# Eight experts' products: weight blocks or token tiles as the stationary operand of TensorE

## The chip, the cores and the metric

The kernel runs on one core of a Trainium2 chip. Its time is device time in microseconds (us) of one launch; lower is better. TensorE (PE) multiplies a stationary operand, which a LDWEIGHTS instruction puts into the array first (PEld), by a moving operand that is streamed through it column by column, and writes the sums to the eight PSUM banks of 128 x 512 float32. VectorE (DVE), ScalarE (ACT) and GpSimd (POOL) do the rest, and SyncE (SP) issues most transfers. All data are float32. In the trace each float32 product stands as two LDWEIGHTS and two MATMUL records with the same shapes: two halves of one product.

## The reference

Three layers run one after the other on 256 tokens of width 1024. The change touches only the mixture of experts of the second layer: a router picks two of eight experts for each token, each expert is a gated network with 3584 hidden columns, and the results come back weighted.

```
def moe_swiglu(h, w_router, b_router, w_gate, w_up, w_down):
    logits = (t @ w_router).astype(jnp.float32) + b_router.astype(jnp.float32)
    top_v, top_e = lax.top_k(logits, TOP_K)
    gate = jax.nn.softmax(top_v, axis=-1)
...
    def one(args):
        xb, e = args
        return (jax.nn.silu(xb @ w_gate[e]) * (xb @ w_up[e])) @ w_down[e]
```

The matrices of one expert are gate and up, 1024 x 3584 each, and down, 3584 x 1024. With eight experts that is most of what the kernel reads.

## The kernel before, in words

Each expert has CAP = 96 token slots, three groups of 32 (GRP = 3). Weights pass through a ring of six slots of 2 MB (slabs). SP issues a slab's transfer as soon as TensorE has freed the slot it goes to (issue, line 164), always in the order in which TensorE uses them; TensorE waits for a slab at its first use (slab). All of TensorE's products in this stage are issued by the helper mm, so they carry line 183.

For each expert TensorE runs two waves: 16 blocks of 128 hidden columns, then 12 (for the last expert 11; the block left over is computed in a loop of steps at the end, which also takes the tokens beyond 96 slots). A wave is expand for gate (banks 0 to 2), then expand for up (banks 3 to 5). The order for an expert is gate and up of wave 0, gate and up of wave 1, contract (down) of wave 0, locate (two products that find which tokens the next expert takes), contract of wave 1.

In expand the stationary operand is a 128 x 32 tile of tokens, moe_he, and the moving operand is a strided run of up to 512 weight columns (chunk). Four such products, one for each quarter of the array's columns (cg), write four quarters of the partitions of a bank. The result has tokens and weight columns mixed so that VectorE's 32 x 32 transposes can turn it: VectorE multiplies silu(gate) by up into moe_act (line 2784) and transposes that into moe_actT (line 2788). In contract moe_actT, 128 x 32, is again stationary, and 256 columns of down weights move, four quarters beside each other, into banks 6 and 7.

ScalarE applies silu (line 2629), copies bank 6 out (line 2619) and stores the expert's rows in four transfers (line 2622). VectorE copies bank 7 out (line 2673). The next expert's tokens come by locate, three small VectorE steps that end in the index (lines 2663 to 2665), an indirect transfer issued by GpSimd (line 2861), and three transposes into moe_he (line 2655); TensorE waits for them (he_ready) before the next expert's first product. During expert 0 four batches of spread products (moe_rows) are put between the phases and copied out by ScalarE.

The order of the work is that of the code: no planner sets it. The code of the stage is the function experts:

Of the kernel before, what the change touches and what calls it, by code (L numbers as in the profile page):

```python
# [19 lines left out]
P = 128  # L20
# [2171 lines left out]

def plan_experts(m):
# [12 lines left out]


class Experts:
# [3 lines left out]
    def __init__(self, m, ctx):  # L2212
# [20 lines left out]
        self.slot = sb("slot", [P, GRP])  # L2233
        self.pos, self.g = sb("pos", [P, TT, 8]), sb("g", [P, TT, 8])
        self.count = sb("count", [1, 8])
        self.rowT = sb("rows", [8, 2, T])
# [3 lines left out]
        self.selT = sb("selT", [P, GRP, T])  # L2240
        self.he = sb("he", [P, 2, GRP, KD, 32])
        self.sg = sb("silu", [P, GRP, 512])
        self.act = sb("act", [P, GRP, 512])
        self.actT = [sb(f"actT{w}", [P, GRP, nb, 32]) for w, (b0, nb) in enumerate(WAVES)]
        self.ye = sb("ye", [P, GRP, T])
# [157 lines left out]
class Routes:  # L2403
# [3 lines left out]
    def __init__(self, m, x, ctx):  # L2407
# [5 lines left out]
        self.diag = x.selT[:, 0:TT, 0:P]  # L2413
# [6 lines left out]
def experts(m, x, prep, router, rt):  # L2420
# [4 lines left out]
    G, U, DN = m.bank[0:3], m.bank[3:6], m.bank[6:8]  # L2425
    SC, LAST_SC = [m.bank[i] for i in range(4)], [m.bank[i] for i in range(4, 8)]
    chunk = lambda ap, cg, nb: ap.rearrange("p (b c r) -> p c b r", c=4, r=32)[:, cg]
    gath, he_ready, g_ready, sg_ready, u_ready, mul_done, at_ready, d_done, ye_ready, sc_ready, added, sel_ready, selT_ready, \
# [8 lines left out]
    a = m.a  # L2437

# [4 lines left out]
    half = GRP * 2  # L2443
    with nc.Block() as block:
        @block.tensor
        def _(pe):
# [56 lines left out]
            def scatter(e):  # L2503
                pe.wait_ge(ye_ready.sem, 2 * (e + 1))
                pe.wait_ge(selT_ready.sem, 1)
                for hf in range(2):
                    for g in range(GRP):
                        for cg in range(4):
                            r = slice(32 * cg, 32 * cg + 32)
                            end = hf == 1 and g == GRP - 1 and cg == 3  # L2510
                            m.mm(pe, LAST_SC[cg][:, hf * T:(hf + 1) * T], x.ye[r, g, hf * P:(hf + 1) * P], x.selT[r, g, :],
                                 g == 0, g == GRP - 1, sc_ready if end else None, skip_group_check=True)

            def spread(n):

                for j in range(4):
                    e = (n % 2) * 4 + j
                    m.mm(pe, DN[j // 2][:, (j % 2) * T:(j % 2 + 1) * T], m.onehot[0:8, e, :], x.rowT[:, n // 2, :], True, True,
                         sp_ready if j == 3 else None)
# [14 lines left out]
            for i, src in enumerate((x.pos, x.g)):  # L2534
                for t in range(TT):
                    c = i * T + t * P
                    m.mm(pe, m.bank[6][0:8, c:c + P], src[:, t, :], m.ident[:], True, True,
# [3 lines left out]
            for e in range(N_EXPERTS):  # L2541
                pe.wait_ge(he_ready.sem, e + 1)
                expand("eg", e, 0, G, g_ready)
                if e == 0:
                    pe.wait_ge(rows_out.sem, 1)
                    pe.wait_ge(rt.rb_out.sem, 1)
                    spread(0)
                expand("eu", e, 0, U, u_ready)
                if e == 0:
                    pe.wait_ge(sp_out.sem, 1)  # L2550
                    spread(1)
                pe.wait_ge(sg_ready.sem, half * e + GRP)
                expand("eg", e, 1, G, g_ready)
                if e == 0:
                    pe.wait_ge(sp_out.sem, 2)
                    spread(2)
                pe.wait_ge(mul_done.sem, half * e + GRP)
                expand("eu", e, 1, U, u_ready, 0, 2)
                if e == 0:
                    pe.wait_ge(sp_out.sem, 3)  # L2560
                    spread(3)
                expand("eu", e, 1, U, u_ready, 2, 4)
                if e == 0:
                    pe.wait_ge(sp_out.sem, 4)
                else:
                    pe.wait_ge(ye_ready.sem, 2 * e)
                pe.wait_ge(at_ready.sem, half * e + GRP)
                contract(e, 0)
                pe.wait_ge(mul_done.sem, half * e + half)
                pe.wait_ge(sg_ready.sem, half * e + half)  # L2570
                if e + 1 < N_EXPERTS:
                    locate(e + 1)
                if e == LAST:
                    bring()
                pe.wait_ge(at_ready.sem, half * e + half)
# [18 lines left out]
        def _(act):  # L2594
            def spread_out(n):
                act.wait_ge(sp_ready.sem, n + 1)
                for j in range(2):
                    ins = act.activation(x.spread[:, n // 2, (n % 2) * 4 + 2 * j:(n % 2) * 4 + 2 * j + 2, :],
                                         DN[j][:].rearrange("p (e n) -> p e n", e=2), ACT.Copy)
                ins.then_inc(sp_out.sem, 1)  # L2600
# [12 lines left out]
            act.activation(x.rowT[:], m.bank[6][0:8, :].rearrange("p (a n) -> p a n", a=2), ACT.Copy).then_inc(rows_out.sem, 1)  # L2613
            for e in range(N_EXPERTS):
                if e:
                    act.wait_ge(d_done.sem, e)
                    if e >= 2:
                        act.wait_ge(written.sem, 64 * (e - 1))
                    act.activation(x.ye[:, 0:2, :], DN[0][:].rearrange("p (g n) -> p g n", g=2), ACT.Copy).then_inc(ye_ready.sem, 1)  # L2619
                    act.wait_ge(ye_ready.sem, 2 * e)  # L2620
                    for cg in range(4):
                        act.dma_start(x.y_rows[(e - 1) * CAP:e * CAP, cg * T:(cg + 1) * T].rearrange("(g r) n -> r g n", r=32),
                                      x.ye[32 * cg:32 * cg + 32]).then_inc(written.sem, 16)
                for w, (b0, nb) in enumerate(waves(e)):
                    act.wait_ge(g_ready.sem, 2 * e + w + 1)
                    if e or w:
                        act.wait_ge(mul_done.sem, half * e + GRP * w)
                    for g in range(GRP):
                        act.activation(x.sg[:, g, 0:32 * nb], G[g][:, 0:32 * nb], ACT.Silu).then_inc(sg_ready.sem, 1)  # L2629
                    if e == 0:  # L2630
                        spread_out(2 * w)
                        spread_out(2 * w + 1)
# [5 lines left out]
            act.wait_ge(written.sem, 64 * LAST)  # L2638
            act.activation(x.ye[:, 0:2, :], DN[0][:].rearrange("p (g n) -> p g n", g=2), ACT.Copy).then_inc(ye_ready.sem, 1)
# [5 lines left out]
        def _(v):  # L2645
# [22 lines left out]
            def combine(e):  # L2668

                v.wait_ge(d_done.sem, e + 1)  # L2670
                if e:
                    v.wait_ge(written.sem, 64 * e)
                v.tensor_copy(x.ye[:, 2, :], DN[1][:, 0:T]).then_inc(ye_ready.sem, 1)
                if e < LAST:
                    return
                v.wait_ge(sp_out.sem, 4)
                for g in range(GRP):
                    ins = v.scalar_tensor_tensor(out=x.selT[:, g, :], in0=x.spread[:, 0, e, :], scalar=x.slot[:, g:g + 1],
                                                 in1=x.spread[:, 1, e, :], op0=ALU.is_equal, op1=ALU.mult)
                ins.then_inc(selT_ready.sem, 1)  # L2680
# [34 lines left out]
            def plan_steps():  # L2715

                wide = lambda ap: ap.rearrange("p (a c) -> p a c", a=1).broadcast_to([1, N_EXTRA, N_EXPERTS])
                nf = D_FFE // P
                v.memset(x.rank[:], 1.0)
# [52 lines left out]
            for e in range(N_EXPERTS):  # L2772
# [5 lines left out]
                for w, (b0, nb) in enumerate(waves(e)):  # L2778
                    v.wait_ge(u_ready.sem, 2 * e + w + 1)
                    if e or w:  # L2780
                        v.wait_ge(at_ready.sem, half * e + GRP * w)
                    for g in range(GRP):
                        v.wait_ge(sg_ready.sem, half * e + GRP * w + g + 1)
                        v.tensor_tensor(x.act[:, g, 0:32 * nb], x.sg[:, g, 0:32 * nb], U[g][:, 0:32 * nb], ALU.mult)\  # L2784
                            .then_inc(mul_done.sem, 1)
                    for g in range(GRP):
                        v.wait_ge(mul_done.sem, half * e + GRP * w + g + 1)
# [1457 lines left out]
```

## Time and profile before

| what | value |
|---|---|
| time, median of 3 runs | 2288.18 us (2286.75 to 2290.34) |
| time of the profiled execution | 2291.82 us |
| its span, first to last instruction | 2290.1 us |
| mean granted TensorE clock | 0.985 of full speed |
| PE, PEld busy | 2216.6 us (97%), 1579.4 us (69%) |
| DVE, ACT, POOL busy | 883.7 us (39%), 393.3 us (17%), 169.4 us (7%) |
| read from HBM | 532.94 MB |

The expert stage runs from about 858 to 1756 us of the span. PE's busy time is the union of its matmuls' spans. A matmul's span is longer than the distance from its start to the next one's, since matmuls are pipelined, so what a matmul costs in a stream is the distance from start to start, and a mean span does not tell it. The busy time of a group divided by its count comes near to that distance.

### The profile page before, as it was taken

How to read it: one execution, taken by the hardware profiler on the slowest of the kernel's cores; microseconds unless marked ns; L12 is line 12 of the kernel's file. 1: busy time of each engine (PE TensorE's matmuls, PEld its weight loads, DVE VectorE, ACT ScalarE, POOL GpSimd, SP SyncE). 2: the span in 40 equal slices, each digit the busy share in tenths (PEclk: the TensorE clock that was granted, in tenths of full speed). 3: DMA queues.
4: the chain of work that ended last, by engine and by line, in shares of the span. 5: the costliest groups of instructions: out<-in, count | busy, mean ns of one | idle time of the engine just before them, and what ended most of it. 6: DMA issues, size and time to landing. Idle time of an engine off the chain costs nothing. (4 is left out here: it accounts for less than half of the span.)

```text
span 2290.1 us, 49032 instructions
## 1 busy us (share of the span) xinstructions
PE 2216.6 (97%) x22096; PEld 1579.4 (69%) x22096; DVE 883.7 (39%) x1657; ACT 393.3 (17%) x822; POOL 169.4 (7%) x250
## 2 busy tenths in 40 slices
PE   8999999999999999999999999999998999899998
PEld 7699889998689973535353534344446877689997
DVE  2676455452566431010000100111013374768764
ACT  0242311100233320000000010000001342224302
POOL 1000100000000012000000000000001162400000
PEclk9999999999999999999999999999999997899999
DMA  7423354434333377999999999999997211055440
GB/s 248 148 93 130 122 210 158 162 129 166 111 108 123 102 276 281 403 387 393 416 411 417 413 411 414 409 415 408 415 404 261 94 38 39 10 189 187 148 182 20
DMA packets 170559, 540.96 MB, mean 236 GB/s; under 512 B 17068, under 2 KB 35022, under 8 KB 153966
## 3 DMA queue, kind: packets, MB, share of 16 engines
q1 hardware_dynamic: 154144, 528.81, 60.0%
q10 hardware_dynamic: 14622, 4.16, 0.8%
q0 software_dynamic: 1584, 4.85, 0.5%
q8 instruction: 174, 2.85, 0.5%
q14 instruction: 35, 0.29, 0.0%
HBM read 532.94 MB, written 4.85 MB: 235 GB/s over the span
## 5 line engine op out<-in xcount | busy, mean ns | idle before, releaser
L183 PE MATMUL bank<-ring,moe_he 128*32 128x512 f32 (+2 forms) x6144 | 577.7, 537 | 2.8 <-DMA ring<-in_moe_w_up 2.7
L183 PEld LDWEIGHTS bank<-ring,moe_he 128*32 128x32 f32 x6144 | 198.7, 110 | 376.6 <-issue 367.7
L183 PE MATMUL bank<-hT,ring 128*128 128x128 f32 (+1 forms) x1952 | 290.7, 307 | 9.7 <-PEq L932 3.4
L183 PE MATMUL bank<-ring,moe_actT 128*32 128x256 f32 x5352 | 292.3, 379 | 1.3 <-DMA ring<-in_moe_w_down 1.3
L183 PEld LDWEIGHTS bank<-hT,ring 128*128 128x128 f32 x1952 | 263.4, 191 | 33.4 <-issue 8.8
L183 PEld LDWEIGHTS bank<-ring,moe_actT 128*32 128x32 f32 x5352 | 174.1, 110 | 116.9 <-issue 3.9
L2784 DVE TENSOR_TENSOR moe_act<-moe_silu,bank 128x512 f32<-128x512 f32 (+2 forms) x48 | 26.8, 614 | 540.4 <-PE bank L183 540.4
L183 PE MATMUL bank<-ring 128*128 128x128 f32 (+2 forms) x976 | 121.8, 284 | 1.4 <-ACT ring L826 1.4
L183 PEld LDWEIGHTS bank<-ring 128*128 128x128 f32 (+1 forms) x976 | 115.8, 190 | 4.0 <-ACT ring L826 1.8
L183 PE MATMUL bank<-kept,ring 128*128 128x256 f32 (+1 forms) x448 | 96.6, 378 | 6.1 <-PEq L1709 3.0
L183 PEld LDWEIGHTS bank<-kept,ring 128*128 128x128 f32 x448 | 83.2, 198 | 18.5 <-issue 5.4
L2629 ACT ACTIVATE moe_silu<-bank 128x512 f32<-128x512 f32 (+2 forms) x48 | 22.6, 542 | 410.7 <-PE bank L183 410.7
L183 PE MATMUL bank<-ffn_sums,ring 128*128 128x128 f32 x768 | 88.4, 275 | 0.0
L183 PE MATMUL bank<-cffn_sums,ring 128*128 128x128 f32 x768 | 88.4, 275 | 0.0
L183 PEld LDWEIGHTS bank<-ffn_sums,ring 128*128 128x128 f32 x768 | 87.0, 192 | 0.0
L183 PEld LDWEIGHTS bank<-cffn_sums,ring 128*128 128x128 f32 x768 | 87.0, 192 | 0.0
L2861 POOL DMA_INDIRECT ring<-h_rows,moe_index x21 | 20.2, 960 | 723.5 <-DVE moe_index L2665 719.2
L1630 DVE TENSOR_TENSOR ring<-ring 128x1024 f32<-128x1024 f32 (+1 forms) x52 | 59.3, 1159 | 19.6 <-PE bank L183 18.2
L2619 ACT ACTIVATE moe_ye<-bank 128x512 f32<-128x512 f32 x7 | 4.2, 598 | 346.7 <-PE bank L183 346.7
L1636 DVE TENSOR_TENSOR ring<-ring 128x1024 f32<-128x1024 f32 (+1 forms) x52 | 59.4, 1161 | 9.8 <-PE bank L183 8.8
L1633 DVE TENSOR_TENSOR ring<-ring 128x1024 f32<-128x1024 f32 (+1 forms) x52 | 59.2, 1158 | 0.5
L183 PE MATMUL bank<-merged,ring 128*128 128x256 f32 x256 | 56.1, 380 | 0.0
(841 smaller groups left out, 2553.1 us busy)
## 6 DMA issues: line engine op xcount, KB each, us to landing
ring<-in_moe_w_down SPq DMA_DIRECT2D x55, 2048.0 KB, 19.1
ring<-in_moe_w_gate SPq DMA_DIRECT2D x32, 2048.0 KB, 23.2
ring<-in_moe_w_up SPq DMA_DIRECT2D x32, 2048.0 KB, 22.8
ring<-in_w_in SPq DMA_DIRECT2D x29, 2048.0 KB, 8.0
ring<-in_moe_w_gate SPq DMA_DIRECT2D x28, 1536.0 KB, 18.1
ring<-in_moe_w_up SPq DMA_DIRECT2D x28, 1536.0 KB, 14.6
ring<-in_w_up SPq DMA_DIRECT2D x10, 2048.0 KB, 11.9
ring<-in_w_out SPq DMA_DIRECT2D x6, 2048.0 KB, 7.9
```

The costliest lines, as they stand in the source:

```text
L183: ins = pe.matmul(out, lhsT, rhs, start=start, stop=stop, **kw)
L1630: return v.tensor_tensor(self.t3, self.b[1, 1], self.b[0, 1], ALU.subtract)
L1633: return v.tensor_tensor(self.b[0, 1], self.b[0, 1], self.b[0, 0], ALU.subtract)
L1636: return v.tensor_tensor(self.t2, self.t3, self.b[0, 0], ALU.add)
L2619: act.activation(x.ye[:, 0:2, :], DN[0][:].rearrange("p (g n) -> p g n", g=2), ACT.Copy).then_inc(ye_ready.sem, 1)
L2629: act.activation(x.sg[:, g, 0:32 * nb], G[g][:, 0:32 * nb], ACT.Silu).then_inc(sg_ready.sem, 1)
L2784: v.tensor_tensor(x.act[:, g, 0:32 * nb], x.sg[:, g, 0:32 * nb], U[g][:, 0:32 * nb], ALU.mult)\
L2861: g.indirect_dma_start(x.picked[:, j, :], None, x.rows_of_h, bass.IndirectOffsetOnAxis(ap=x.index[:, e % 2, j:j + 1], axis=0)).then_inc(pi ...
```

## The change

The token slots and the weights change places in expand. A block of 128 x 128 weights is now stationary, and the 96 token slots move, so the result has hidden columns on the partitions and 96 slots along the row: the layout that down needs, with no transpose. Four blocks fill 384 columns of a bank (PIECE = 4). Wave 0 needs four banks each for gate and up, so bank 6 joins gate and bank 7 joins up, and the products into gate's fourth bank wait until the previous expert's results have been copied out (ye_ready). In contract a tile of 128 columns of moe_actT (96 slots and 32 columns that belong to the next block, or zeros at the end) is stationary, and 512 columns of down weights move, twice for a block. The results are plain rows of 1024, stored with one transfer. The spread products of expert 0 are gathered in two places and use eight half-filled steps of other banks. The last scatter uses the whole array, and its mask is one VectorE instruction where it was three.

```
+    G, U, DN = m.bank[0:3] + m.bank[6:7], m.bank[3:6] + m.bank[7:8], m.bank[6:8]
...
-                        for g in range(GRP):
-                            for cg in range(4):
-                                end = k == KD - 1 and g == GRP - 1 and cg == 3
-                                m.mm(pe, banks[g][32 * cg:32 * cg + 32, 0:32 * nb], x.he[:, e % 2, g, k, :],
-                                     chunk(s[:, kk, :], cg, nb), k == 0, k == KD - 1, ready if end else None,
-                                     skip_group_check=True)
+                        for b in range(nb):
+                            if key == "eg" and e and k == 0 and b // PIECE == 3 and b % PIECE == 0:
+                                pe.wait_ge(ye_ready.sem, 2 * e)
+                            c = b % PIECE * CAP
+                            m.mm(pe, banks[b // PIECE][:, c:c + CAP], s[:, kk, b * P:(b + 1) * P], x.he[:, e % 2, :, k, :],
+                                 k == 0 and c == 0, k == KD - 1, ready if k == KD - 1 and b == nb - 1 else None,
+                                 skip_group_check=True)
...
-                    for g in range(GRP):
-                        for cg in range(4):
-                            first, last = w == 0 and b == 0, w == 1 and b == nb - 1
-                            end = last and g == GRP - 1 and cg == 3
-                            m.mm(pe, DN[g // 2][32 * cg:32 * cg + 32, (g % 2) * T:(g % 2 + 1) * T], x.actT[w][:, g, b, :],
-                                 s[:, b % 4, cg * T:(cg + 1) * T], first and g % 2 == 0, last, d_done if end else None,
-                                 skip_group_check=True)
+                    for h in range(2):
+                        first, last = w == 0 and b == 0, w == 1 and b == nb - 1
+                        m.mm(pe, DN[h][:], x.actT[w][:, b * CAP:b * CAP + P], s[:, b % 4, h * 512:(h + 1) * 512], first, last,
+                             d_done if last and h else None, skip_group_check=True)
...
-                    for g in range(GRP):
-                        v.wait_ge(mul_done.sem, half * e + GRP * w + g + 1)
-                        v.transpose(x.actT[w][:, g, 0:nb, :].rearrange("p b n -> p (b n)"), x.act[:, g, 0:32 * nb])\
-                            .then_inc(at_ready.sem, 1)
+                    for i, b in enumerate(range(0, nb, PIECE)):
+                        n = min(PIECE, nb - b) * CAP
+                        v.wait_ge(sg_ready.sem, pieces(e, w - 1) + i + 1)
+                        v.tensor_tensor(x.actT[w][:, b * CAP:b * CAP + n], x.silu[:, b:b + n // CAP, :].rearrange("p b n -> p (b n)"),
+                                        U[i][:, 0:n], ALU.mult).then_inc(mul_done.sem, 1)
```

On PE, experts 0 and 1 read like this before (-) and now (+). The last two numbers are the columns of the stationary and of the moving operand, and x96 counts products in a row; moe_he and moe_actT are the token tiles, ring holds the weights, moe_sel is locate, and moe_rows is the spread.

```order
+L183 MATMUL bank<-moe_he,ring 128x96 x448
+L183 MATMUL bank<-moe_rows,onehot 128x256 x6
+L183 MATMUL bank<-ring,moe_actT 128x512 x32
 L183 MATMUL bank<-moe_sel,ring 128x96 x2
-L183 MATMUL bank<-ring,moe_actT 32x256 x144
-L183 MATMUL bank<-ring,moe_he 32x512 x192
-L183 MATMUL bank<-ring,moe_he 32x384 x192
-L183 MATMUL bank<-ring,moe_actT 32x256 x192
+L183 MATMUL bank<-moe_rows,onehot 128x256 x10
+L183 MATMUL bank<-ring,moe_actT 128x512 x24
+L183 MATMUL bank<-moe_he,ring 128x96 x448
+L183 MATMUL bank<-ring,moe_actT 128x512 x32
```

An expert's 384 expand products of 128 x 32 tiles are now 448 with a 128 x 128 block each, and the 336 down products, 192 of wave 0 and 144 of wave 1, are 56 with 512 moving columns, 32 and 24. The two locate products stand where they stood.

On DVE, where TensorE's phases are waited for, the rows of expert 2 before are these:

```order
L2784 TENSOR_TENSOR moe_act<-moe_silu,bank 128x512 x3
L2788 STREAM_TRANSPOSE moe_actT<-moe_act 128x512 x3
L2795 TENSOR_SCALAR moe_sel<-moe_iota,moe_pos 128x96 x2
L2784 TENSOR_TENSOR moe_act<-moe_silu,bank 128x384 x3
L2788 STREAM_TRANSPOSE moe_actT<-moe_act 128x384 x3
```

And these are the rows of the same expert now, down to the copy of its results:

```order
L2775 TENSOR_TENSOR moe_actT<-moe_silu,bank 128x384 x4
L2782 TENSOR_SCALAR moe_sel<-moe_iota,moe_pos 128x96 x2
L2775 TENSOR_TENSOR moe_actT<-moe_silu,bank 128x384 x3
L2657 TENSOR_TENSOR moe_found<-bank,moe_diag 128x96
L2658 TENSOR_REDUCE moe_where<-moe_found 128x3
L2659 TENSOR_SCALAR moe_index<-moe_where,moe_part 128x3
L2649 STREAM_TRANSPOSE moe_he<-ring 128x256 x3
L2667 COPY moe_ye<-bank 128x512
```

The transposes into moe_actT are gone, the products with silu come in seven pieces of 384 columns where they were six, and the copy of the down results is 512 columns wide where it was 256.

## Rows read from the trace of the kernel before

**Rows 1.** The page: PE in 40 slices of the span, its clock, the DMA engines.
```profile
PE   8999999999999999999999999999998999899998
PEclk9999999999999999999999999999999997899999
DMA  7423354434333377999999999999997211055440
```

**Rows 2.** Windows view, expert stage: busy us (instructions) by engine; PEclk, DMA share, GB/s.
```profile
core 0: us, PE busy (x) PEld busy (x) DVE busy (x) ACT busy (x) POOL busy (x), PEclk, DMA share, GB/s
1000.00:1700.00 700.00, 697.19 (x9162) 298.82 (x9156) 69.51 (x182) 29.09 (x55) 20.83 (x22) 1.00 1.01 408
```

**Rows 3.** Waits of PE in the stage, by what ended them: us, times, longest.
```profile
PE bank L183 <- DMA ring<-in_moe_w_up: 2.7, 2, 1.5
PE bank L183 <- DMA ring<-in_moe_w_down: 1.3, 3, 0.5
```

**Rows 4.** Timeline of PE, expert 2: start us, us, engine, operands, stationary, moving, count.
```profile
1084.54 72.34 PE L183 MATMUL bank<-ring,moe_he 128*32 128x512 f32 x768
1156.70 20.90 PE L183 MATMUL bank<-ring,moe_actT 128*32 128x256 f32 x384
1177.53 0.69 PE L183 MATMUL bank<-moe_sel,ring 128*128 128x96 f32 x4
1178.15 15.75 PE L183 MATMUL bank<-ring,moe_actT 128*32 128x256 f32 x288
1193.71 6.62 PE L183 MATMUL bank<-ring,moe_he 128*32 128x512 f32 x60
```

**Rows 5.** PE by form, whole span: stationary, moving, count, busy us, mean ns.
```profile
L183 PE MATMUL bank<-ring,moe_he 128*32 128x512 f32 x3072 | 332.0, 592 | 2.8 <-DMA ring<-in_moe_w_up 2.7
L183 PE MATMUL bank<-cffn_sums,ring 128*128 128x128 f32 x768 | 88.4, 275 | 0.0
```

**Rows 6.** Windows view, the last dense layer, where whole 128 x 128 tiles are stationary.
```profile
2070.00:2235.00 165.00, 165.00 (x1481) 165.00 (x1480) 121.49 (x201) 41.33 (x86) 0.00 (x0) 1.00 0.45 160
```

**Rows 7.** PE by form in that window (groups cover 1477 of its 1481).
```profile
L183 PE MATMUL bank<-cffn_sums,ring 128*128 128x128 f32 x680 | 78.4, 275 | 0.0
L183 PE MATMUL bank<-hT,ring 128*128 128x128 f32 x400 | 46.5, 275 | 0.0
L183 PE MATMUL bank<-cffn_act,ring 128*128 128x128 f32 x237 | 28.4, 275 | 0.0
L183 PE MATMUL bank<-cffn_act_sums,ring 128*128 128x128 f32 x160 | 18.8, 275 | 0.0
```

**Rows 8.** Timeline of PE: 8 columns moving; 512 columns moving; the last scatter.
```profile
851.02 0.59 PE L2528 MATMUL bank<-route_mask,ones 128*128 128x8 f32 x4
...
59.62 13.04 PE L183 MATMUL bank<-ring,hT 128*128 128x512 f32 x30
...
1755.84 2.87 PE L183 MATMUL bank<-moe_selT,moe_ye 32*128 32x256 f32 x48
```

**Rows 9.** Timeline of DVE at the end of expert 3.
```profile
1287.43 0.26 DVE L2663 TENSOR_TENSOR moe_found<-bank,moe_diag 128x96 f32<-128x96 f32 x1 [18.41 <-PE bank L183]
1298.46 1.10 DVE L2655 STREAM_TRANSPOSE moe_he<-ring 128x256 f32<-128x256 f32 x3 [10.22 <-DMA ring<-h_rows,moe_index]
1303.19 0.42 DVE L2673 COPY moe_ye<-bank 128x256 f32<-128x256 f32 x1 [0.17 <-PE bank L183]
```

**Rows 10.** DVE by form, 1000 to 1700 us: the products that read a bank.
```profile
L2784 DVE TENSOR_TENSOR moe_act<-moe_silu,bank 128x512 f32<-128x512 f32 x21 | 13.2, 683 | 282.2 <-PE bank L183 282.2
```

**Rows 11.** Slab transfers issued from 1100 to 1650 us: count, KB, median us to landing.
```profile
ring<-in_moe_w_down SPq DMA_DIRECT2D x35, 2048.0 KB, 19.9
ring<-in_moe_w_gate SPq DMA_DIRECT2D x20, 2048.0 KB, 24.2
ring<-in_moe_w_up SPq DMA_DIRECT2D x20, 1536.0 KB, 14.7
```

**Rows 12.** Windows view, before and after the clock fell in the last layer.
```profile
1896.30:1903.10 6.80, 6.18 (x89) 5.21 (x90) 4.61 (x12) 2.83 (x8) 6.23 (x7) 1.00 0.01 2
1903.10:1916.70 13.60, 13.60 (x106) 9.94 (x103) 6.03 (x14) 2.38 (x9) 2.90 (x4) 0.50 0.01 2
```

More of the change, by code:

```diff
@@ L2190, in waves, with pieces @@
     return WAVES if e < N_EXPERTS - 1 else (WAVES[0], (16, 11))
+PIECE = 4
+PIECES = sum(-(-nb // PIECE) for _, nb in WAVES)
+def pieces(e, w):
+    return PIECES * e + sum(-(-nb // PIECE) for _, nb in WAVES[:w + 1])
 def plan_experts(m):
@@ L2232, in __init__ @@
         self.second = spare[:, 2 * D:3 * D]
-        self.slot = sb("slot", [P, GRP])
+        self.slot = sb("slot", [P, 1])
         self.pos, self.g = sb("pos", [P, TT, 8]), sb("g", [P, TT, 8])
         self.count = sb("count", [1, 8])
-        self.rowT = sb("rows", [8, 2, T])
+        self.rowT = sb("rows", [P, 2, T])
         self.spread = sb("spread", [P, 2, N_EXPERTS + 1, T])
@@ L2437, in experts @@
     a = m.a
+    SPREAD = (0, 1, 2, 0, 1, 2, 3, 5)
     def count(eng):
@@ L2505, in scatter, with spread @@
                 pe.wait_ge(selT_ready.sem, 1)
-                for hf in range(2):
-                    for g in range(GRP):
[L2508 to L2519, printed above, removed]
+                for c in range(KD):
+                    m.mm(pe, LAST_SC[c // 2][:, c % 2 * T:(c % 2 + 1) * T], x.ye[:, c * P:(c + 1) * P], x.selT[:], True, True,
+                         sc_ready if c == KD - 1 else None)
+            def spread(units):
+                for u in units:
+                    for j in range(2):
+                        m.mm(pe, m.bank[SPREAD[u]][:, j * T:(j + 1) * T], m.onehot[:, u % 4 * 2 + j, :], x.rowT[:, u // 4, :],
+                             True, True, sp_ready if j else None)
             pe.wait_ge(rt.consts.sem, 1)
@@ L2546, in _ @@
                     pe.wait_ge(rt.rb_out.sem, 1)
-                    spread(0)
                 expand("eu", e, 0, U, u_ready)
-                if e == 0:
[L2550 to L2558, printed above, removed]
+                pe.wait_ge(sg_ready.sem, pieces(e, 0))
+                expand("eg", e, 1, G, g_ready)
+                pe.wait_ge(mul_done.sem, pieces(e, 0))
+                expand("eu", e, 1, U, u_ready)
+                pe.wait_ge(sg_ready.sem, pieces(e, 1))
+                if e == 0:
+                    spread(range(3))
+                    pe.wait_ge(pads_zero.sem, 3)
+                contract(e, 0)
+                pe.wait_ge(mul_done.sem, pieces(e, 1))
+                if e + 1 < N_EXPERTS:
+                    locate(e + 1)
                 if e == 0:
                     pe.wait_ge(sp_out.sem, 3)
[L2561 to L2572, printed above, removed]
+                    spread(range(3, len(SPREAD)))
                 if e == LAST:
                     bring()
-                pe.wait_ge(at_ready.sem, half * e + half)
                 contract(e, 1)
@@ L2594, in _, with spread_out @@
         def _(act):
[L2595 to L2600, printed above, removed]
+            def spread_out(u):
+                act.wait_ge(sp_ready.sem, u + 1)
+                e = u % 4 * 2
+                act.activation(x.spread[:, u // 4, e:e + 2, :], m.bank[SPREAD[u]][:].rearrange("p (e n) -> p e n", e=2),
+                               ACT.Copy).then_inc(sp_out.sem, 1)
             for q in range(4):
@@ L2612, in _ @@
             act.wait_ge(rows_ready.sem, 1)
-            act.activation(x.rowT[:], m.bank[6][0:8, :].rearrange("p (a n) -> p a n", a=2), ACT.Copy).then_inc(rows_out.sem, 1)
+            act.wait_ge(pads_zero.sem, 1)
+            act.activation(x.rowT[0:8], m.bank[3][0:8, :].rearrange("p (a n) -> p a n", a=2), ACT.Copy).then_inc(rows_out.sem, 1)
             for e in range(N_EXPERTS):
@@ L2617, in _ @@
                     if e >= 2:
[L2618 to L2619 removed]
+                        act.wait_ge(written.sem, 16 * (e - 1))
+                    act.activation(x.ye[:, 0:512], DN[0][:], ACT.Copy).then_inc(ye_ready.sem, 1)
                     act.wait_ge(ye_ready.sem, 2 * e)
[L2621 to L2623 removed]
+                    act.dma_start(x.y_rows[(e - 1) * CAP:e * CAP, :], x.ye[0:CAP, :]).then_inc(written.sem, 16)
                 for w, (b0, nb) in enumerate(waves(e)):
@@ L2626, in _ @@
                     if e or w:
[L2627 to L2632, printed above, removed]
+                        act.wait_ge(mul_done.sem, pieces(e, w - 1))
+                    for i, b in enumerate(range(0, nb, PIECE)):
+                        n = min(PIECE, nb - b)
+                        act.activation(x.silu[:, b:b + n, :], G[i][:, 0:n * CAP].rearrange("p (b n) -> p b n", b=n), ACT.Silu)\
+                            .then_inc(sg_ready.sem, 1)
+                if e == 0:
+                    for u in range(len(SPREAD)):
+                        spread_out(u)
                 if e == 1:
@@ L2671, in combine @@
                 if e:
-                    v.wait_ge(written.sem, 64 * e)
-                v.tensor_copy(x.ye[:, 2, :], DN[1][:, 0:T]).then_inc(ye_ready.sem, 1)
+                    v.wait_ge(written.sem, 16 * e)
+                v.tensor_copy(x.ye[:, 512:D], DN[1][:]).then_inc(ye_ready.sem, 1)
                 if e < LAST:
                     return
[L2676 to L2680, printed above, removed]
+                v.scalar_tensor_tensor(out=x.selT[:], in0=x.spread[:, 0, e, :], scalar=x.slot[:, 0:1], in1=x.spread[:, 1, e, :],
+                                       op0=ALU.is_equal, op1=ALU.mult).then_inc(selT_ready.sem, 1)
             def find_pairs():
@@ L2832, in _ @@
                           allow_small_or_imprecise_dtypes=True), rt.consts)
-            k.step(g.iota(x.slot[:], pattern=[[32, GRP]], base=0, channel_multiplier=1,
-                          allow_small_or_imprecise_dtypes=True))
-            for c in range(1, 4):
-                k.step(g.tensor_scalar(x.slot[32 * c:32 * c + 32, :], x.slot[32 * c:32 * c + 32, :], -32.0 * c, None, ALU.add))
+            k.step(g.memset(x.rowT[:], 0.0), pads_zero)
+            for w, (b0, nb) in enumerate(WAVES):
+                k.step(g.memset(x.actT[w][:, nb * CAP:], 0.0), pads_zero)
+            k.step(g.iota(x.slot[:], pattern=[[0, 1]], base=0, channel_multiplier=1, allow_small_or_imprecise_dtypes=True))
+            k.step(g.memset(x.slot[CAP:P, :], -8.0))
             for i in range(2):
@@ L2882, in _ @@
             m.clear_last(sp)
-            sp.wait_ge(at_ready.sem, half * N_EXPERTS)
+            sp.wait_ge(mul_done.sem, PIECES * N_EXPERTS)
             sp.wait_ge(weighed.sem, 2)
```

33 lines of the change are left out of this document (14 added, 19 removed).

## The prediction

> **What bounds the kernel now.** I read the slices first. PE stands at 9 tenths or more almost throughout, but from 860 to 1740 us the DMA engines stand at 9 too [rows 1]: two candidates for the bound. The windows view gives both in numbers: from 1000 to 1700 us PE is busy 697.19 of 700 us and the DMA engines are full as well, 408 GB/s at a share of 1.01, while DVE and ACT have 10% and 4% [rows 2]. The waits decide between the two. In the stage TensorE waits for weights 2.7 + 1.3 = 4.0 us in all [rows 3]. Nearly all the time, then, it is TensorE that paces: SP can issue a slab only when TensorE frees its slot. But the transfers are close behind. A slab takes 14.7 to 24.2 us from issue to landing [rows 11], and with six slots it is wanted about five slab times after its issue, that is 5 x 5.2 = 26 us (the 21 slabs' worth of an expert in 109.17 us, next paragraph). So a cheaper TensorE would gain almost nothing here, while a dearer one is paid in full. The question is only which it is.
>
> One expert is read from the timeline: it begins at 1084.54, the next at 1193.71, so 109.17 us: 72.2 us of expand, 20.8 of down, 0.62 of locate (1177.53 to 1178.15), 15.6 of down [rows 4]. There is no hole in it. The spans of single matmuls mislead here: 592 ns is the mean span with 512 columns, but 3072 of them fill 332.0 us, 108 ns each [rows 5], because four run side by side on the quarters of the array. Four take 432 ns, which is 0.84 ns per streamed column.
>
> **Expand now.** For an expert, 2 matrices x 8 row tiles x 28 blocks = 448 products, as the order of instructions shows, each recorded as two halves: 896 instructions, each with its own load of 128 x 128 weights and 96 moving columns. What does one cost in a stream? Streaming alone would be 96 x 0.84 = 81 ns. But each wants a new 128-column load. The last dense layer runs just that load with 128 moving columns: 1481 matmuls in 165.00 us [rows 6], all but four of them of that form [rows 7], so 111.4 ns each, and PEld is busy all the time. 128 x 0.84 is 107.5, so that row alone can't say if load or stream sets the pace. Two short rows say it. Four matmuls that move only 8 columns span 0.59 us [rows 8]; with a last span of 0.26, which is my reading of what an almost empty matmul takes (0.59 less three gaps), three gaps of 0.11 remain. And the four locate matmuls, 128 x 128 stationary and exactly 96 columns moving, span 0.69 us; less a last one of 0.275, the span that the 128-column form has [rows 7], and less their first gap, which is not pipelined, this is again about 0.11 for each of the others [rows 4]. So the load is a floor of 111 ns, whatever moves. I take 111.4. The bounds: 107.5 below (the load at the pace of a column) and 88.4/768 = 115.1 above [rows 5].
>
> 896 x 0.1114 = 99.8 us for an expert, where expand took 72.2. The work per column is the same as before (four quarters of 32 tokens against 96 slots on the whole array); what is added is that each load now serves 96 columns where its stream would be shorter than itself.
>
> The Trainium skill, in "TensorE: Matmul & The Clock Gate", section "Back-to-back issue gap", gives about 81 ns for each matmul in a sustained stream of loads and matmuls with 128 columns. By that, expand would be 896 x 0.081 = 73 us, an estimate from the page. The float32 rows of this case have 111.4 ns for that shape, so the measurement decides. The same page, section "LDWEIGHTS (loading the stationary operand)", says that a load goes by its columns at 1.2 per ns, so 107 ns for 128, and this agrees with the 8-column row.
>
> **Down now.** 28 blocks x 2 halves of the row x 2 = 112 instructions, each with 512 columns. Thirty matmuls of this shape span 13.04 us [rows 8]; less a last span of 0.59 [rows 5] and over 29 gaps that is 0.429 us. Loads of 111 ns hide under it. 112 x 0.429 = 48.1 us, where down took 20.8 + 15.6 = 36.4: a third more, because the stationary tile has 128 columns of which only 96 are slots, where three groups of 32 wasted nothing. The upper bound is 13.04/30 = 0.435; the lower is the pace of the expand groups before, 72.2 us over 96 groups of 512 and 96 of 384 columns, 0.839 ns a column, 0.430, so no lower.
>
> **Sum for an expert.** 99.8 + 48.1 + 0.6 (locate, as before) = 148.5, against 109.17: 39.3 more. Seven experts: 275. The last has 27 blocks of 28: 38. Together +313.
>
> **What goes away or moves beside it.** The 4.0 us of waits for weights [rows 3] go: an expert's 44.0 MB (15 slabs of 2048 KB and 8 of 1536 [rows 11]) over 148.5 us are 297 GB/s, well below the 408 that the engines are seen to carry [rows 2]. So -4. The DVE transposes go; DVE was waiting for PE anyway (282 us of idle time ahead of its products [rows 10]), so nothing. ACT's silu in pieces of 384 and the four stores that become one: nothing, ACT has 96% free [rows 2]. The spread products of expert 0 are 16 as before, with the same 256 columns; two batches instead of four save perhaps 1 us of joins. The last scatter had 2.87 us [rows 8]; it becomes 16 instructions of 256 columns, 16 x 256 x 0.84 = 3.4 us, +0.6, and two mask instructions fewer lie under the loop of steps. The memsets on POOL come before the first silu is wanted; nothing.
>
> Two waits could newly show. First, the next expert's tokens: from locate's end at 1287.4 to the end of the transposes at 1299.6 takes 12.1 us [rows 9]. Behind locate now lie 48 x 0.429 = 20.6 us of down (before: 15.6). It has more cover than it had. Second, gate's fourth bank: TensorE now waits for the copies of banks 6 and 7 after 12 blocks, 24 x 0.111 = 2.7 us into the next expert. Behind that wait stands the whole stream of TensorE, and so SP's slots. The copies begin at once after the last down product (1303.19, with 0.17 of idle time [rows 9]); a 512-column read of a bank takes DVE about 0.68 us [rows 10]. That is under 1 us against 2.7: nothing. If VectorE's extra work after experts 3 and 5 delayed it, it would be 1 to 4 us once; it ran before 1303.19 in expert 3 and has 5 us more now. The upper bound is 3 us at each of seven experts, +20.
>
> Sum: 313 - 4 - 1 + 0.6 = +309. The profiled execution took 2291.82 us with a span of 2290.1, so 2600.8; the median is 3.6 us below that execution, so I forecast **2597 us**, 13.5% more.
>
> **The rivals.**
> - The load hides. If the background load is free of the stream and the 8-column rows are only short bursts, an instruction costs its 81 ns. Expand is then 72.6 us an expert, about what it was, and only down grows: +11.7 an expert, 2597 - 7136 x 0.0304 = 2380 us (7136 is 896 x 7 + 864). For it: the locate rows are few and never more than four in a row. Against it: 1481 in a row at 111.4 with PEld never idle, and the 8-column row. 4%.
> - The load is in the open. If loads don't run ahead when the stream is shorter, an instruction costs 111 + 81 = 192 ns, and the time is 2597 + 7136 x 0.081 = 3175 us. Against it: three of four locate matmuls. 3%.
> - The clock falls. It has fallen to 0.50, of the two levels 1.2 and 2.4 GHz the lower, after 6.8 us in which 89 small matmuls ran [rows 12]; in the new expand the array streams 81 of 111 ns, far more than there, and in down all the time. At half clock all through expand the time would be near 2597 + 795 = 3390 us. 2%.
> - Not slower. The stage is paced by the transfers (DMA share 1.01 [rows 2]) and TensorE's records, whose ends are modelled, only stretch over the waiting. Then each expert lasts 44.0 MB / 408 GB/s = 107.9 us as long as TensorE needs less, about 2278 us in all. It decides at (107.9 - 48.1 - 0.6) / 896 = 66 ns for an expand instruction, below even the pure stream of 81. Also the distance of 108 ns for four-abreast matmuls equals the pace of columns elsewhere (0.84 against 0.429/512), so they aren't stretched. 2%.
> - The forecast holds but a new wait of several us comes at every expert (the copies, the tokens, slab waits that break the run of loads): 2640 to 2700 us. 4%.
> The forecast itself has 85%.
>
> **How the numbers follow.** The range takes the bounds of the unknown costs: 7136 x (107.5 - 111.4) = -28 to 7136 x (115.1 - 111.4) = +26 us for the load, +5 for down (892 x 0.006), up to +20 for the copies, not all at once. I give 2568 to 2640. What lies outside is the rivals, about 15%. Two runs of this kernel can tell 0.2% (5 us). Slower by over that holds in all but the fourth rival: slower 0.98, same 0.01, faster 0.01.
>
> **What would show it.** In the profile after: expand groups of 896 instructions that last about 100 us, with PEld busy through them and 111 ns from start to start; down groups of 64 and 48 that last 27.5 and 20.6 us; an expert every 148.5 us; DMA near 0.7 and 297 GB/s, slabs landing in well under 20 us; no waits of PE for the copies; PEclk at 1.00. Wrong is: an expert in under 125 us (the load hides), over 155 us (a new wait, whose releaser the waits will name), or granted clock below 0.95 in the stage.

## The result, and the profile after

The changed kernel takes 2592.72 us (median of 4 runs, 2585.08 to 2598.12) against 2287.47 us (4 runs, 2285.07 to 2290.34): 1.133 times the time before, 95% interval 1.130 to 1.136. The forecast was 2597 us in a range of 2568 to 2640. The profiled execution has a span of 2591.7 us, 301.6 more than before.

The first view is the timeline of PE in the expert stage after, which answers to [rows 4]: start us, us, engine, line, operands, stationary, moving, count.

```profile
1139.79 20.79 PE L183 MATMUL bank<-ring,moe_actT 128*128 128x512 f32 x48
1160.42 100.19 PE L183 MATMUL bank<-moe_he,ring 128*128 128x96 f32 x896
1260.44 27.66 PE L183 MATMUL bank<-ring,moe_actT 128*128 128x512 f32 x64
1287.94 0.58 PE L183 MATMUL bank<-moe_sel,ring 128*128 128x96 f32 x4
1288.35 20.79 PE L183 MATMUL bank<-ring,moe_actT 128*128 128x512 f32 x48
1308.98 21.24 PE L183 MATMUL bank<-moe_he,ring 128*128 128x96 f32 x189
```

An expert lasts from 1160.42 to 1308.98, 148.56 us, without a hole. The starts divide it: 100.0 us of expand, 27.5 of down, 0.4 of locate, 20.6 of down. Before they were 72.2, 20.8, 0.6 and 15.6. From start to start an expand instruction takes 100.02/896 = 111.6 ns.

The second is the list of groups by form of the whole span, PE and then PEld: count, busy us, mean ns of one, idle time of the engine just before. It answers to [rows 5].

```profile
L183 PE MATMUL bank<-moe_he,ring 128*128 128x96 f32 x7136 | 798.0, 275 | 0.0
L183 PE MATMUL bank<-ring,moe_actT 128*128 128x512 f32 x892 | 385.8, 593 | 0.0
...
L183 PEld LDWEIGHTS bank<-moe_he,ring 128*128 128x128 f32 x7136 | 798.0, 192 | 3.4 <-issue 3.3
L183 PEld LDWEIGHTS bank<-ring,moe_actT 128*128 128x128 f32 x892 | 168.4, 190 | 205.8 <-issue 205.7
```

Expand: 798.0 us over 7136 are 111.8 ns each, and PEld is busy for the same 798.0 us. Down: 385.8/892 = 432 ns each, and there PEld is idle for 205.8 us, more than half the time, so the stream sets the pace. A PEld that is always busy does not prove by itself that the load sets the pace, since the spans of loads overlap too (192 ns each at 111.8 ns from one to the next); the runs below decide that. The mean span of a matmul (275 ns) tells nothing here: it is the same as with 128 moving columns [rows 7].

The windows view of a stretch inside one expand, and of the stage, after; columns as in [rows 2].

```profile
1165.00:1255.00 90.00, 90.00 (x809) 90.00 (x808) 2.30 (x6) 4.59 (x10) 0.00 (x0) 1.00 0.79 286
...
1000.00:1700.00 700.00, 700.00 (x4918) 586.16 (x4917) 34.99 (x115) 24.80 (x50) 11.34 (x12) 1.00 0.84 302
```

The 809 matmuls in 90 us are 111.2 ns apart (the count takes in two or three that were under way at the edge, which is why the starts give 111.6). The DMA share fell from 1.01 to 0.84 and the rate from 408 to 302 GB/s. The slabs land much sooner, as the list of issues from 1100 to 1900 us after shows (KB, median us to landing), which answers to [rows 11].

```profile
ring<-in_moe_w_down SPq DMA_DIRECT2D x39, 2048.0 KB, 9.1
ring<-in_moe_w_gate SPq DMA_DIRECT2D x24, 2048.0 KB, 7.9
...
ring<-in_moe_w_up SPq DMA_DIRECT2D x20, 1536.0 KB, 6.5
```

The same three kinds took 14.7 to 24.2 us before. In the waits of PE no slab appears in the stage any more, and no copy of the banks. DVE copies its half of the results of expert 1 (bank 7) at the start of expert 2:

```profile
1160.62 0.69 DVE L2667 COPY moe_ye<-bank 128x512 f32<-128x512 f32 x1 [10.77 <-PE bank L183]
```

It ends at 1161.31. ScalarE's copy of bank 6 starts at 1160.62 as well and takes 0.60 us. TensorE waits for both copies 24 instructions into the expert, at 1160.42 + 2.7 = 1163.1, so the margin is 1.8 us.

### The profile page after: what moved, and what is told of

The parts are those of the page before. It is cut to its first block and busy times, and to the rows that moved or that the text cites. A ratio compares the mean times of both kernels' runs of the same rounds, so it can differ in the third digit from the quotient of the medians.

```text
span 2591.7 us, 41962 instructions
## 1 busy us (share of the span) xinstructions
PE 2524.5 (97%) x18596; PEld 2172.1 (84%) x18596; DVE 856.7 (33%) x1615; ACT 394.2 (15%) x830; POOL 169.0 (7%) x251
## 5 line engine op out<-in xcount | busy, mean ns | idle before, releaser
L183 PEld LDWEIGHTS bank<-moe_he,ring 128*128 128x128 f32 x7136 | 798.0, 192 | 3.4 <-issue 3.3
L183 PE MATMUL bank<-moe_he,ring 128*128 128x96 f32 x7136 | 798.0, 275 | 0.0
L183 PE MATMUL bank<-ring,moe_actT 128*128 128x512 f32 x892 | 385.8, 593 | 0.0
L183 PEld LDWEIGHTS bank<-ring,moe_actT 128*128 128x128 f32 x892 | 168.4, 190 | 205.8 <-issue 205.7
L2775 DVE TENSOR_TENSOR moe_actT<-moe_silu,bank 128x384 f32<-128x384 f32 (+1 forms) x56 | 27.3, 547 | 764.8 <-PE bank L183 764.8
L2622 ACT ACTIVATE moe_silu<-bank 128x384 f32<-128x384 f32 (+1 forms) x56 | 23.1, 493 | 604.9 <-PE bank L183 604.9
```

The source lines that it names most:

```text
L183: ins = pe.matmul(out, lhsT, rhs, start=start, stop=stop, **kw)
L2622: act.activation(x.silu[:, b:b + n, :], G[i][:, 0:n * CAP].rearrange("p (b n) -> p b n", b=n), ACT.Silu)\
L2775: v.tensor_tensor(x.actT[w][:, b * CAP:b * CAP + n], x.silu[:, b:b + n // CAP, :].rearrange("p b n -> p (b n)"), U[i][:, 0:n], ALU.mult).t ...
```

## The experiments

Each was timed beside the kernel before on the same chip. Ratios are to that kernel, with 95% intervals. An edit is shown against the changed kernel, unless its section says that it starts from the kernel before; "..." marks what is left out.

### New expand, old down

```
-                    for h in range(2):
-                        m.mm(pe, DN[h][:], x.actT[w][:, b * CAP:b * CAP + P], s[:, b % 4, h * 512:(h + 1) * 512], ...
+                    for g in range(GRP):
+                        for cg in range(4):
+                            m.mm(pe, DN[g // 2][32 * cg:32 * cg + 32, (g % 2) * T:(g % 2 + 1) * T],
+                                 x.actT[w][:, b * CAP + 32 * g:b * CAP + 32 * g + 32],
+                                 s[:, b % 4, cg * T:(cg + 1) * T], ...
```

> Only expand has the 128 x 128 weight blocks as stationary; down, its copies, stores and the last scatter are those of the kernel before. My theory (a load of 128 columns costs 111.4 ns in a stream, whatever moves): expand adds 27.6 us to each of seven experts and 26.6 to the last, less the 4 us of waits for weights: 2287.5 + 220 - 4 = about 2503 us, with an expert in 136.8 us. Rival (the new layout of down, or a wait at the hand-over of the banks, carries a good part): under 2460 or over 2540 us.

The copies, stores and last scatter of the kernel before go with it. Measured: 2508.12 us (4 runs, 2504.0 to 2510.22), ratio 1.097 (1.094 to 1.100); before 2286.08. That is +222 us. The timeline of PE of this kernel:

```profile
1138.06 100.29 PE L183 MATMUL bank<-moe_he,ring 128*128 128x96 f32 x896
1238.28 20.93 PE L183 MATMUL bank<-ring,moe_actT 128*32 128x256 f32 x384
1259.13 0.69 PE L183 MATMUL bank<-moe_sel,ring 128*128 128x96 f32 x4
1259.75 15.75 PE L183 MATMUL bank<-ring,moe_actT 128*32 128x256 f32 x288
1275.43 100.29 PE L183 MATMUL bank<-moe_he,ring 128*128 128x96 f32 x896
```

An expert is 137.37 us: the new 100.2 and the old 37.2. The theory had 136.8 and 2503. Here one wait appeared that the full change does not have, after expert 5, where VectorE has preparatory work before its copy (PE's timeline, then DVE's):

```profile
1692.83 27.44 PE L183 MATMUL bank<-moe_he,ring 128*128 128x96 f32 x229 [2.37 <-DVE moe_ye L2677]
```
```profile
1684.80 1.10 DVE L2659 STREAM_TRANSPOSE moe_he<-ring 128x256 f32<-128x256 f32 x3 [12.02 <-DMA ring<-h_rows,moe_index]
...
1692.35 0.42 DVE L2677 COPY moe_ye<-bank 128x256 f32<-128x256 f32 x1
```

TensorE stood 2.37 us for the copy. So the hand-over of the banks is a live hazard of the change. In the full version the same copy comes in time:

```profile
1754.94 0.69 DVE L2667 COPY moe_ye<-bank 128x512 f32<-128x512 f32 x1 [4.42 <-issue]
```

VectorE was through with the preparatory work 4.42 us before this copy could start. Two things gave it that room. Down of the second wave lasts 20.6 us instead of 15.7; by the times of the run above that alone would have been enough (an estimate). And the next expert's tokens, for which VectorE waits before this work, came 8 us after their index instead of 12.

### Old expand, new down

This edit starts from the kernel before.

```
-                            m.mm(pe, DN[g // 2][32 * cg:32 * cg + 32, (g % 2) * T:(g % 2 + 1) * T], x.actT[w][:, g, b, :],
-                                 s[:, b % 4, cg * T:(cg + 1) * T], ...
+                        m.mm(pe, DN[h][:], x.actT[w][:, b * CAP:b * CAP + P], s[:, b % 4, h * 512:(h + 1) * 512], ...
...
-                        v.transpose(x.actT[w][:, g, 0:nb, :].rearrange("p b n -> p (b n)"), x.act[:, g, 0:32 * nb])\
+                        v.transpose(x.actT[w][:, 0:nb * CAP].rearrange("p (b n) -> p b n", n=CAP)[:, :, 32 * g:32 * g + 32], ...
```

> Only down has the whole tiles of 128 columns as stationary and 512 weight columns moving; expand is that of the kernel before, and the VectorE transposes stay and write into the new layout. My theory (down pays for 128 columns where 96 are slots): 11.7 us for an expert, 8 x 11.7 - 4 = +90: about 2377 us, an expert in 120.8 us. Together with the run beside it the parts add up to the whole change. Rival (a 512-column stream hides something else and down is no dearer): about 2287 us.

Measured: 2372.13 us (4 runs, 2370.21 to 2379.16), ratio 1.038 (1.035 to 1.041), +86 us. Its timeline of PE:

```profile
1106.00 72.37 PE L183 MATMUL bank<-ring,moe_he 128*32 128x512 f32 x768
1178.30 27.73 PE L183 MATMUL bank<-ring,moe_actT 128*128 128x512 f32 x64
...
1206.29 20.79 PE L183 MATMUL bank<-ring,moe_actT 128*128 128x512 f32 x48
1227.01 72.37 PE L183 MATMUL bank<-ring,moe_he 128*32 128x512 f32 x768
```

121.01 us an expert, 120.8 expected. The two halves add to 222 + 86 = 308 us, and the whole change costs 2592.72 - 2287.47 = 305. The medians carry a scatter of a few us, so no interplay of weight shows between the halves.

### A shorter stream under the same load

```
-                            m.mm(pe, banks[b // PIECE][:, c:c + CAP], s[:, kk, b * P:(b + 1) * P], x.he[:, e % 2, :, k, :],
+                            n = 2 if k else GRP
+                            m.mm(pe, banks[b // PIECE][:, c:c + (32 * n)], s[:, kk, b * P:(b + 1) * P], x.he[:, e % 2, 0:n, k, :],
```

> The changed kernel, but in expand only 64 of the 96 token slots move for seven of the eight row tiles (the third group of 32 is left out there). Load floor: 6244 instructions keep their 111.4 ns, the time stays at 2593 us within 5. If the stream of columns had a part in the price: at 64 x 0.84 = 54 ns of stream, a sum of load and stream would lose 27 ns each, 170 us: 2423 us.

Measured: 2595.4 us (2 runs), ratio 1.135 (1.132 to 1.139). The groups by form of this kernel:

```profile
L183 PE MATMUL bank<-moe_he,ring 128*128 128x64 f32 x6244 | 701.6, 275 | 0.0
```

A third of the streamed columns is gone in seven of the eight row tiles, and nothing is gained: the same 100.0 us for each expand (from 1159.82 to 1259.82 in this kernel's timeline). 701.6/6244 gives 112.4 ns, a little too much, because the groups of 64 and of 96 columns alternate and each adds the whole span of its last matmul (275 ns) where the next one starts after 112.

### A shorter load under the same stream

```
-                            m.mm(pe, banks[b // PIECE][:, c:c + CAP], s[:, kk, b * P:(b + 1) * P], x.he[:, e % 2, :, k, :],
+                            n = 64 if k else P
+                            m.mm(pe, banks[b // PIECE][0:n, c:c + CAP], s[:, kk, b * P:b * P + n], x.he[:, e % 2, :, k, :],
```

> The changed kernel, but in expand only 64 of a block's 128 columns are loaded for seven of the eight row tiles (half of the results lack those parts), and the 96 slots move as before. Load floor: the load takes about half, some 56 ns, so the stream of 96 columns sets the pace: 81 to 83 ns an instruction, 6244 x 0.029 = 181 us less: about 2412 us. If the price were a fixed cost of an instruction with a full array: no change, 2593 us. If the loads were in the open: 56 + 81 = 137 ns, 2750 us.

Measured: 2423.18 us (2 runs), ratio 1.060 (1.057 to 1.063), 170 us less than the changed kernel where 181 were expected. PE and PEld by form:

```profile
L183 PE MATMUL bank<-moe_he,ring 128*64 128x96 f32 x6244 | 522.0, 246 | 0.0
...
L183 PEld LDWEIGHTS bank<-moe_he,ring 128*64 128x64 f32 x6244 | 516.0, 137 | 3.0
```

522.0/6244 = 83.6 ns: the pace of 96 columns (81) plus a little, which the last section takes apart. With the run before it this settles what an instruction costs here: the longer of the two, load or stream, and not their sum. At 128 loaded columns that is the load, at 64 the stream. PEld is busy for 516.0 of 522.0 us here too, though the stream sets the pace: a busy PEld does not name the bound.

### TensorE made cheap in the kernel before

This edit starts from the kernel before too.

```
-                        for g in range(GRP):
+                        for g in range(GRP - 1):
                             for cg in range(4):
-                                end = k == KD - 1 and g == GRP - 1 and cg == 3
+                                end = k == KD - 1 and g == GRP - 2 and cg == 3
```

> The kernel before, but expand leaves out the third group of 32 token slots in all eight experts: a third of its matmuls, 24.1 us an expert less work for TensorE (85 us an expert are left). It measures where the stage would go if TensorE were cheap. My theory (the transfers are just behind): the time falls only to the pace of the transfers, 44.0 MB at 408 to 418 GB/s = 105 to 108 us an expert against 109.2, and somewhat more in the first expert, where the DMA engines were not yet full: 2245 to 2275 us. Rival (TensorE alone paces, the DMA engines' share of 1.01 is only waiting packets): 8 x 24.1 = 193 us less, 2093 us.

Measured: 2265.32 us (5 runs, 2258.87 to 2267.93), ratio 0.991 (0.988 to 0.994); before 2286.68. Of 193 us taken from TensorE, 21 came out of the time. The timeline and the waits (us in total, times, longest) of PE, and the windows view:

```profile
1107.92 2.79 PE L183 MATMUL bank<-ring,moe_he 128*32 128x384 f32 x32 [0.94 <-DMA ring<-in_moe_w_gate]
1111.69 2.79 PE L183 MATMUL bank<-ring,moe_he 128*32 128x384 f32 x32 [0.98 <-DMA ring<-in_moe_w_gate]
```
```profile
PE bank L183 <- DMA ring<-in_moe_w_up: 70.2, 55, 3.4
PE bank L183 <- DMA ring<-in_moe_w_gate: 48.4, 44, 2.4
PE bank L183 <- DMA ring<-in_moe_w_down: 18.2, 8, 2.7
```
```profile
1000.00:1700.00 700.00, 575.52 (x7584) 257.81 (x7580) 70.11 (x182) 29.09 (x55) 20.77 (x22) 0.97 1.02 411
```

TensorE now waits at 99 of the 128 slabs of expand and 8 of the 56 of down, 136.8 us in all where it was 4.0 [rows 3]. The DMA engines stand at a share of 1.02 and 411 GB/s, and the kernel before was already at 1.01 and 408 [rows 2].

The two locate products of each expert show where the 21 us were won. These are the first and the seventh of this kernel, then those of the kernel before:

```profile
933.32 0.69 PE L183 MATMUL bank<-moe_sel,ring 128*128 128x96 f32 x4
...
1591.97 0.69 PE L183 MATMUL bank<-moe_sel,ring 128*128 128x96 f32 x4
```
```profile
959.19 0.69 PE L183 MATMUL bank<-moe_sel,ring 128*128 128x96 f32 x4
...
1614.22 0.69 PE L183 MATMUL bank<-moe_sel,ring 128*128 128x96 f32 x4
```

From the start of the stage to the first locate this kernel takes 77.2 us (856.13 to 933.32) and the kernel before 101.2 (from 857.95): all of the 24.1 us that were taken out of expert 0 are won. The six experts behind it take 658.65 us here and 655.03 before, 109.8 and 109.2 each: a third less of expand, and nothing won. So the expectation was right in its time and in its first expert, but the 105 to 108 us for each of the others were not reached. In the steady part TensorE and the transfers need the same time for an expert, to within 1%. The granted clock was 0.97 in the window above, which costs TensorE a part of what it was spared, but with the DMA engines full it does not set the pace.

### Down with 96 loaded columns

```
-                        m.mm(pe, DN[h][:], x.actT[w][:, b * CAP:b * CAP + P], s[:, b % 4, h * 512:(h + 1) * 512], first, last,
+                        n = P if first else CAP
+                        m.mm(pe, DN[h][0:n, :], x.actT[w][:, b * CAP:b * CAP + n], s[:, b % 4, h * 512:(h + 1) * 512], first, last,
```

> The changed kernel, but the stationary tile of down has 96 columns instead of 128 in all blocks but the first of an expert; the 512 columns that move stay. My theory (down costs its stream of 2 x 2 x 512 columns a block, the width of the tile is free): no change, 2593 us within 5. Rival (the third that down is dearer by is paid for the 32 columns without slots): down falls by up to a quarter, 8 x 12 = 96 us less, 2497 us.

Measured: 2593.19 us (4 runs, 2592.23 to 2597.97), ratio 1.136 (1.131 to 1.140). The 48 instructions of a second wave:

```profile
1287.54 20.77 PE L183 MATMUL bank<-ring,moe_actT 128*96 128x512 f32 x48
```

20.77 us against 20.79: the width of the tile does not enter. Down is a third dearer because a block now streams 2 x 512 columns through the array one after the other, where three groups sent 256 each through all four quarters at once, 768 in all: 1024/768 = 4/3, and 48.1/36.4 is 1.32. Leaving the 32 spare columns of the tile out saves nothing.

## Why the prediction was right

**What bounds the kernel.** "A cheaper TensorE would gain almost nothing here, while a dearer one is paid in full": shown from both sides. Cheaper by 193 us gave 21; dearer by 39.4 us an expert gave all of it. One row was read too widely: the DMA engines stand at 9 tenths from 916 us on, and at 7 in the slices before it, which hold the first 57 us of the stage [rows 1]. That is the one place where a cheaper TensorE gained.

**Expand.** 99.8 us an expert were forecast, 100.0 measured. The step that carried the forecast was to take the price from rows of the load and not of the stream, and the two runs that shorten one and then the other show that it was the load. The three rows behind it (1481 matmuls with 128 columns, four with 8, four with 96) made this likely and did not prove it: in the first the two prices nearly agree, and the other two are bursts of four with an assumed last span. One of the arguments against "the load hides" has no weight: that PEld was never idle holds also in the run with 64 loaded columns (516.0 of 522.0 us), where the load does hide.

**Down.** 48.1 forecast, 27.5 + 20.6 = 48.1 measured. Locate took 0.4 us where 0.6 were forecast ("as before"): its products no longer stand between 32-wide tiles, which the last section prices. That happens to cancel the 0.2 by which expand was short.

**The sum.** From the first expand of expert 0 to the loop of steps, the stage took 885.99 us before and takes 1193.12: +307.1 against the +309 of the forecast. The timelines show the ends, first those of after, then those of before.

```profile
856.27 100.29 PE L183 MATMUL bank<-moe_he,ring 128*128 128x96 f32 x896
956.40 2.78 PE L183 MATMUL bank<-moe_rows,onehot 128*128 128x256 f32 x12
...
986.90 4.51 PE L183 MATMUL bank<-moe_rows,onehot 128*128 128x256 f32 x20
...
2049.39 3.72 PE L2577 MATMUL bank<-hT,moe_silu 128*128 128x256 f32 x16 [1.40 <-issue]
```
```profile
857.95 20.81 PE L183 MATMUL bank<-ring,moe_he 128*32 128x512 f32 x192
878.68 1.99 PE L183 MATMUL bank<-moe_rows,onehot 8*128 8x256 f32 x8
...
1743.94 3.71 PE L2583 MATMUL bank<-hT,moe_silu 128*128 128x256 f32 x16 [1.39 <-issue]
```

The spread products in two batches take 2.6 + 4.4 = 7.0 us by their starts; in four they took 1.9 each, 7.7: the "perhaps 1 us" was 0.7. The other 5.5 us between 307.1 and the span's 301.6 lie outside the stage, 1.7 of them before its first product. They fit the granted clock, which is 1.00 through the stage in both traces and below that outside it: the mean is 0.985 over 2290.1 us before and 0.989 over 2591.7 after, so 0.015 x 2290.1 = 34 and 0.011 x 2591.7 = 29 us of full clock are missing, an estimate from these four numbers. The spread of the runs goes with it too: beside the experiments the kernel before took 2277.1 to 2277.8 us in the three runs at 0.991, and 2287.0 to 2291.4 in the six at 0.983 to 0.986. No run was made to test this.

**The waits.** Neither showed in the full change. For the copies, under 1 us against 2.7 was worked out, and 0.9 us against 2.7 measured. In the run with the old down, where 15.7 us of cover were left instead of 20.6, VectorE's work after expert 5 did delay its copy, and TensorE waited 2.4 us. The forecast allowed 1 to 4 us for that.

**The transfers.** 297 GB/s were forecast; 302 in the window. "DMA near 0.7" was too low: the share is 0.84. Scaling 1.01 by the rates gives 0.74, and the share falls by less than the rate, because a packet's time is not constant: on the queue of the slabs 40441 packets took 98.8% of the 16 engines' time from 1100 to 1650 us before, 0.215 us each, and 43971 took 82.2% from 1100 to 1900 us after, 0.239 us each, at nearly the same size (5.5 and 5.4 KB).

**The rivals.** "The load hides" (2380 us) and "the load is in the open" (3175 us) fell with the time itself. The 64-column stream, which gained nothing, and the 64-column load, which left the pace of the stream, show the mechanism. The clock stayed at 1.00 through the stage, but the argument for that was a poor one: of the 89 matmuls before the fall [rows 12], 16 were not small (256 columns each, 3.7 us together), and PE was busy for 6.18 of 6.80 us, so the rows do not show that expand keeps the array far busier. "Not slower" fell with the first timeline. Its premise was half true, though: from the second expert on the transfers need as long for an expert as TensorE (109.8 us in the run with the cheap TensorE, 109.2 before). The new wait at every expert did not come.

No run here beats the kernel before while it computes all of the result. The run with the cheap TensorE suggests that cheaper products alone could win some 20 us in this stage, as long as all weights are read, and those only in its first expert.

## What to carry to other kernels

When stationary and moving operand change places, count the loads as well as the columns. For float32 on the whole array each instruction cost the longer of its load and its stream here: 111.6 ns for 128 loaded columns, with 64, 96 or 128 columns moving, and about 0.84 ns for each moving column where the stream was longer. So with a whole block of 128 stationary, a moving side under 128 columns is paid as 128. Four 32-wide tiles side by side, each with a stream of 512 columns (432 ns for the four), keep the load out of the way, and waste nothing when the tokens are a multiple of 32 but not of 128.

Before anything is made cheaper, leave a part of its work out in one run and time that. It tells how far the next bound is away, and the timeline by expert tells where.

## What the runs showed of the hardware that I had not expected

Halving the load to 64 columns brought the price down only to 83.6 ns where the stream alone was put at 81, and an expand took 78.3 us (from 1120.05 to 1198.38 in that kernel's timeline) where 784 x 0.081 + 112 x 0.1114 = 76.0 were worked out. The starts of single matmuls in the traces say where the 2.3 us went.

```profile
1120.05 78.40 PE L183 MATMUL bank<-moe_he,ring 128*128 128x96 f32 x896
1198.38 27.73 PE L183 MATMUL bank<-ring,moe_actT 128*128 128x512 f32 x64
```

A matmul carries a small fixed cost beside its columns. In a run of equal matmuls the starts lie 429.2 ns apart with 512 columns (changed kernel, down), 215.8 with 256 (kernel before, from 77 to 90 us) and 82.5 with 96 behind a 64-column load (this run). The first two differ by 0.833 ns a column, which leaves 2.5 ns, and 96 x 0.833 + 2.5 is the 82.5 of the third. The 0.84 of the forecast was the price of 512 columns with the fixed part spread over them; a short stream pays it in full. Over 784 matmuls that is 784 x 1.5 ns = 1.2 us.

The other 1.2 us are paid where the width of the tile changes, eight times in each expand of this run. From a 128-wide tile to a 64-wide one the next two starts come after 205 and 133 ns, where 112 and 83 are usual, and the other way after 176 and 187 where they are 83 and 112. The step into down, the last of the eight, costs 93 ns. With both parts the sum is 784 x 0.0825 + 112 x 0.1116 + 1.2 = 78.4 us against 78.3. The changed kernel has 128-wide tiles throughout an expert and pays nothing of it. The kernel before pays it around locate, whose four matmuls are followed by the next start after 186, 112, 112 and 205 ns there and after 83, 112, 111 and 112 now: the 0.6 and the 0.4 us.

The same comparison for the load is not possible: 128 columns is the only width at which it set the pace. Its mean spans in the profiles are 110, 137, 163 and 192 ns for 32, 64, 96 and 128 columns, 0.85 ns a column, but what a load costs from start to start was measured at 128 alone.
